# Weighting an expert's results by slot as they leave PSUM, adding them to x2's rows by accumulating gathers, and finishing the last tile in slot order

## The reference, cut to what matters

```python
x = x + hybrid_mixer(rms_norm(x, norm1_g), ...)       # x2 below
xn = rms_norm(x, norm2_g)
# router: best group, the two best experts in it, their weights
combine = sum(one_hot(expert_id, 16) * (g_w * top_p)[..., None], axis=1)
for e in range(16):
    h = silu(xn @ w_gate[e]) * (xn @ w_up[e])          # 1024 -> 512
    y = y + combine[:, e:e + 1] * (h @ w_down[e])      # 512 -> 1024
return rms_norm(x + y, final_norm_g)
```

## Time and profile before

| | |
|---|---|
| median of 3 runs | 788.62 us (787.97 to 789.51) |
| profiled execution, its own time | 789.02 us |
| its span | 787.3 us |
| busy: PE, DVE, ACT, POOL | 764.9 (97%), 492.3 (63%), 450.5 (57%), 209.3 (27%) us |
| DMA | 206.74 MB, mean 263 GB/s |

### The profile page before, as it was taken

The page is one execution under the profiler, slowest core; times in us unless marked ns, Lnnn a source line. Parts: engine busy times, 40 slices in busy tenths (PEclk is TensorE's granted clock), DMA queues, the critical chain, the costliest instruction groups (busy, mean ns, idle before and its releaser), DMA issues.

```text
span 787.3 us, 10839 instructions
## 1 busy us (share of the span) xinstructions
PE 764.9 (97%) x3739; PEld 621.8 (79%) x3739; DVE 492.3 (63%) x702; ACT 450.5 (57%) x590; POOL 209.3 (27%) x124
## 2 busy tenths in 40 slices
PE   7999999999999999999999999999999999999994
PEld 4788777777787888888888788878778888888782
DVE  5704476585743302322022669999999998999888
ACT  5244657566744232323321556787878888888862
POOL 3644433232332444434442532000000000000033
PEclk9999999999999999999999999999999999999998
DMA  8569999792222262332328438999999999999965
GB/s 300 183 213 381 370 337 393 268 342 75 69 66 81 81 214 87 100 107 81 107 97 282 161 131 285 408 409 409 409 409 409 410 409 410 409 409 341 398 251 202
DMA packets 134318, 206.74 MB, mean 263 GB/s; under 512 B 10813, under 2 KB 65669, under 8 KB 134278
## 3 DMA queue, kind: packets, MB, share of 16 engines
q1 hardware_dynamic: 126084, 188.80, 65.7%
q10 hardware_dynamic: 5890, 9.04, 3.1%
q0 software_dynamic: 2304, 8.39, 2.8%
HBM read 157.95 MB, written 48.25 MB: 262 GB/s over the span
## 4 chain that ended last, share of the span: by engine, by line
PE 85%; DVE 6%; ACTq 2%; DMA 2%; POOL 2%; ACT 1%; issue 1%; DVEq 0%; SPq 0%; POOLq 0%
PE ps L1052 25%; PE ps L1054 24%; PE ps L1053 24%; DVE w_lo L389 3%; PE ps L1342 2%; PE ps L1146 1%; PE ps L1174 1%; PE ps L1157 1%; PE ps L1295 1%; POOL raw_mg L656 1%; PE ps L1269 1%; DMA x<-in_x 1%; PE ps L1349 1%; ACTq L877 1%; DMA raw_mg<-slots,slot_idx 1%
## 5 line engine op out<-in xcount | busy, mean ns | idle before, releaser
L383 POOL TENSOR_TENSOR w_lo<-raw,w_hi 128x1024 fp32r<-128x1024 f32 x72 | 174.1, 2422 | 250.4 <-ACT w_hi L371 250.4
L371 ACT ACTIVATE w_hi<-raw 128x1024 fp32r<-128x1024 f32 x73 | 76.8, 1057 | 195.4 <-PE ps L1054 168.0
L1052 PE MATMUL ps<-xn_hi,w_hi 128*128 128x512 f32 x352 | 140.6, 399 | 0.0
L1054 PE MATMUL ps<-xn_hi,w_lo 128*128 128x512 f32 x352 | 137.2, 390 | 0.0
L1053 PE MATMUL ps<-xn_lo,w_hi 128*128 128x512 f32 x352 | 137.1, 390 | 0.0
L1052 PE MATMUL ps<-w_hi,xT_hi 128*128 128x512 f32 (+1 forms) x248 | 97.0, 391 | 2.2 <-DVE w_lo L389 2.2
L1054 PE MATMUL ps<-w_hi,xT_lo 128*128 128x512 f32 (+1 forms) x248 | 95.1, 384 | 0.0
L1053 PE MATMUL ps<-w_lo,xT_hi 128*128 128x512 f32 (+1 forms) x248 | 94.9, 383 | 0.0
L656 POOL DMA_INDIRECT raw_mg<-slots,slot_idx x7 | 7.8, 1113 | 280.4 <-DMA slots<-y_tile 278.5
L1052 PEld LDWEIGHTS ps<-xn_hi,w_hi 128*128 128x128 f32 x352 | 66.1, 188 | 16.2 <-issue 2.0
L1053 PEld LDWEIGHTS ps<-xn_lo,w_hi 128*128 128x128 f32 x352 | 66.1, 188 | 14.1 <-issue 1.0
(11 more groups left out here) (311 smaller groups left out, 1475.1 us busy)
## 6 DMA issues: line engine op xcount, KB each, us to landing
slots<-raw SPq DMA_DIRECT2D x65, 512.0 KB, 7.0
raw<-in_w_in SPq DMA_DIRECT2D x52, 512.0 KB, 4.0
raw_mg<-in_exp_w_down SPq DMA_DIRECT2D x35, 512.0 KB, 11.0
raw<-in_exp_w_gate SPq DMA_DIRECT2D x29, 512.0 KB, 11.3
raw_a<-in_exp_w_gate SPq DMA_DIRECT2D x26, 512.0 KB, 10.6
raw_c<-in_exp_w_up SPq DMA_DIRECT2D x24, 512.0 KB, 11.8
raw_mg<-in_exp_w_up SPq DMA_DIRECT2D x22, 512.0 KB, 11.9
raw<-in_exp_w_up SPq DMA_DIRECT2D x15, 512.0 KB, 11.8
```

What stands on the lines that cost most here:

```text
L371: nc.scalar.activation(w_hi[:, b % HI_SLOTS, :], raw_buf(b), ACT.Copy)\
L383: eng.tensor_tensor(w_lo[:, b % HI_SLOTS, :], raw_buf(b), w_hi[:, b % HI_SLOTS, :].bitcast(F32), ALU.subtract)\
L1052: pe.matmul(dst, hi_l, hi_r, start=start, stop=False)
L1054: return pe.matmul(dst, lo_l, hi_r, start=False, stop=stop)
```

## The change

- Each slot gets a record of four words in a DRAM tensor `info`: the token, its weight, the token's other slot, 0. POOL writes default records, then (once DVE has the weights) the picked slots' records by eight indirect writes, and loads all back to `slot_info`. DVE therefore makes the weights before tile 1.
- `y_part` multiplies by the slot's weight as it copies PSUM to the one buffer `y_home`. It waits for `info_in`. Tile 0's `y_part` comes three splits into the next tile.
- `last_rows_out` (DVE, after tile 4) finds which tokens have a slot in the last tile. POOL writes those tokens' x2 rows in slot order to DRAM (`last_x`) and loads them to `z_home`.
- No tile of zeros. POOL gathers with `compute_op=ALU.add` onto `x_rows`: four before the store of the tile before the last, four after it (and after the first four), and one onto `z_home`.
- The last tile's result is weighted from PSUM onto `z_home` in slot order and normed there; tokens in it are left out when `x_rows` is written. All output rows are written by POOL, by indirect DMA, in five parts.
- PE's and ACT's work with `sel` and the one-hot rows goes, and so do the sums on DVE.

The diff, cut to its core, in the order POOL, ACT, DVE (definitions, then the order of calls):

```diff
-SLOT_TILES = NE * PER_EXPERT + 1
+SLOT_TILES = NE * PER_EXPERT
...
+            pool.iota(slot_info[:, :, 0], pattern=[[0, SLOT_TILES]], base=TOK, channel_multiplier=1)
+            pool.memset(slot_info[:, :, 1:4], 0)
...
+            pool.dma_start(info.rearrange("(p b) n -> p (b n)", p=P), info_words).then_inc(S["info_filled"], 16)
...
             pool.wait_ge(S["routed"], NT + 1)
-            pool.wait_ge(S["y_even_stored"], 16 * (PAIRED // 2 + 1))
-            pool.wait_ge(S["y_odd_stored"], 16 * (PAIRED // 2))
+            for t in range(NT):
+                for k in range(2):
+                    pool.indirect_dma_start(
+                        info, bass.IndirectOffsetOnAxis(ap=info_idx[:, 0, 2 * t + k:2 * t + k + 1], axis=0),
+                        pick_info[:, t, k, :], None).then_inc(S["info_out"], 16)
+            pool.wait_ge(S["info_out"], 16 * 2 * NT)
+            pool.dma_start(info_words, info.rearrange("(p b) n -> p (b n)", p=P)).then_inc(S["info_in"], 16)
+            pool.wait_ge(S["routed"], NT + 2)
+            for t in range(NT):
+                pool.indirect_dma_start(last_x, bass.IndirectOffsetOnAxis(ap=last_places[:, t:t + 1], axis=0),
+                                        x_rows[:, t, :], None, bounds_check=P - 1, oob_is_err=False)\
+                    .then_inc(S["last_x_out"], 16)
...
+            pool.dma_start(z_home, last_x).then_inc(S["z_in"], 16)
...
+            def add_picked(rows, idx, landed_in):
+                pool.indirect_dma_start(rows, None, slots, bass.IndirectOffsetOnAxis(ap=idx, axis=0),
+                                        compute_op=ALU.add).then_inc(landed_in, 16)
+            pool.wait_ge(S["hT_hi_done"], n_stop + (PAIRED - 1))
+            pool.wait_ge(S["y_stored"], n_stop * 16 + 16 * (PAIRED - 1))
+            pool.wait_ge(S["info_in"], 16)
+            pool.tensor_copy(last_info[:, :], info_words[:, bass.ds(last_block * 4, 4)])
+            for t in range(NT):
+                add_picked(x_rows[:, t, :], slot_idx[:, 2 * t:2 * t + 1], S["early_in"])
...
             pool.wait_ge(S["before_last_stored"], 16)
+            add_picked(z_home, last_info[:, 2:3], S["z_in"])
+            pool.wait_ge(S["early_in"], 16 * NT)
             for t in range(NT):
-                gather(0, y_lo(t), t)
-                gather(1, y_hi(t), t)
+                add_picked(x_rows[:, t, :], slot_idx[:, 2 * t + 1:2 * t + 2], rows_in[t])
+            power(0)
+            power(1)
+            power(2)
+            rows_out(0)    
+            power(3)
+            rows_out(1)
+            power(NT)
+            rows_out(2)
+            pool.wait_ge(S["z_norm"], 2)
+            pool.indirect_dma_start(out[0], bass.IndirectOffsetOnAxis(ap=last_info[:, 0:1], axis=0), z_weighed, ...)
+            rows_out(3)
...
-                act.wait_ge(at.y_free, at.y_count)
-                act.activation(at.y, ps[:, 5:7, :].rearrange("p a n -> p (a n)"), ACT.Copy).then_inc(S["y_act"], 1)
+                act.wait_ge(S["info_in"], 16)
+                act.wait_ge(S["y_stored"], at.y_count)
+                act.activation(y_home, ps[:, 5:7, :].rearrange("p a n -> p (a n)"), ACT.Copy,
+                               scale=info_words[:, bass.ds(block * 4 + 1, 1)].bitcast(F32)).then_inc(S["y_act"], 1)
...
+                    if r == 2 and count == SECOND:
+                        y_part(loop_block(1, PER_TILE), at_odd(0), 0)
...
+            y_square(0)
+            y_square(1)
+            y_square(2)
+            z_square(0)
+            y_square(3)
+            z_square(1)
...
+            def info_rows():
+                at = info_idx[:, 0, :]
+                dve.wait_ge(S["routed"], NT)
+                dve.tensor_scalar(at, slot_idx[:, :], P - 1, 6, ALU.bitwise_and, ALU.logical_shift_left)
+                link(dve.tensor_scalar(info_idx[:, 1, :], slot_idx[:, :], 7, None, ALU.logical_shift_right))
+                link(dve.tensor_tensor(at, at, info_idx[:, 1, :], ALU.bitwise_or))
+            def share_of_picks():
+                dve.wait_ge(S["exp_done"], 2)
+                dve.tensor_reduce(g_sum, row(4, NT, NG), AX.X, ALU.add)
+                link(dve.tensor_tensor(mine, where.unsqueeze(2).to_broadcast([P, NT, 2, NE]),
+                                       top_slot[:, :, 0:2].unsqueeze(3).to_broadcast([P, NT, 2, NE]), ALU.is_equal))
+                link(dve.tensor_tensor(mine, mine, share.unsqueeze(2).to_broadcast([P, NT, 2, NE]), ALU.mult))
+                link(dve.tensor_reduce(w_both, mine, AX.X, ALU.add))
+            def last_rows_out():
+                both = top_slot[:, :, 0:2]
+                link(dve.tensor_scalar(in_last, both, last_rows[:, 0:1], None, ALU.is_gt))
+                link(dve.scalar_tensor_tensor(out=in_last, in0=both, scalar=last_rows[:, 1:2], in1=in_last,
+                                              op0=ALU.is_le, op1=ALU.mult))
+                link(dve.scalar_tensor_tensor(out=place_last, in0=both, scalar=last_rows[:, 0:1], in1=in_last,
+                                              op0=ALU.subtract, op1=ALU.mult))
+                link(dve.tensor_reduce(four(8), in_last, AX.X, ALU.add))
+                link(dve.tensor_reduce(four(9), place_last, AX.X, ALU.add))
+                dve.scalar_tensor_tensor(out=out_rows[:, :], in0=four(8), scalar=float(TOK), in1=pick_info[:, :, 0, 0],
+                                         op0=ALU.mult, op1=ALU.add)
...
+                dve.tensor_scalar(last_places[:, :], four(9), float(P), None, ALU.add).then_inc(S["routed"], 1)
+            def gather_order(before):
+                dve.tensor_scalar(before_rows[:, 0:1], block_table[:, bass.ds(before, 1)], float(P), None, ALU.mult)
+                link(dve.tensor_scalar(before_rows[:, 1:2], block_table[:, bass.ds(before, 1)], float(P), float(P),
+                                       ALU.mult, ALU.add))
...
+                dve.scalar_tensor_tensor(out=idx[:, :, 1], in0=at_second, scalar=-1.0, in1=apart,
+                                         op0=ALU.add, op1=ALU.subtract).then_inc(S["routed"], 1)
...
             overflow_count()
-            overflow_tiles(0, block_table, NE * PER_EXPERT)
+            share_of_picks()
             for r in range(AHEAD):
                 split_lo_loop(at_odd(0), r)
...
             hidden(B_EXP + 8, 1)
+            combine_weights()
...
             tile(at_odd(0))
+            overflow_tiles(0, block_table, NE * PER_EXPERT)
             full_tables()
+            tile(at_even(1))
             last_tile()
-            tile(at_even(1))
+            tile(at_odd(1))
             last_tile_rows()
-            gather_swaps()
-            tile(at_odd(1))
-            gather_order()
             tile(at_even(2))
-            share_of(0)
-            share_of(1)
+            last_rows_out()
             tile(at_odd(2))
-            combine_weights()
             dve.wait_ge(S["tab"], 1)
             n_stop = dve.value_load(tile_table[0:1, 0:1], ...)
+            gather_order(n_stop + (PAIRED - 1))
...
+            def z_sum(c):
+                at = slice(512 * c, 512 * (c + 1))
+                dve.wait_ge(S["w_used"], loop_block(tiles, 3 + c))
+                dve.scalar_tensor_tensor(out=z_home[:, at], in0=ps[:, 5 + c, :], scalar=last_info[:, 1:2].bitcast(F32),
+                                         in1=z_home[:, at], op0=ALU.mult, op1=ALU.add).then_inc(S["z_sum"], 1)
+            y_mean(0, 1)
+            y_normed(0)
+            y_mean(1, 2)
+            dve.wait_ge(S["z_in"], 32)
+            z_sum(0)
+            z_sum(1)
+            y_mean(2, 3)
+            y_normed(1)
+            z_weigh(0)
+            y_mean(3, 5)
+            z_weigh(1)
...
+            y_normed(2)
...
+            y_normed(3)
```

More of the change, by code:

```diff
@@ L300, in build @@
         x0_in = [sem(f"x0_in{s}") for s in range(NT)]
-        got_in = [[sem(f"got{k}_in{t}") for t in range(NT)] for k in range(2)]
+        rows_in = [sem(f"rows_in{t}") for t in range(NT)]
         even_buf = ([raw_a[:, n, :] for n in range(3)] + [raw_c[:, n, :] for n in range(4)] + [raw[:, 4, :]]
@@ new lines, in _ @@
+            pool.wait_ge(S["hT_hi_done"], n_stop + (PAIRED - 1))
+            pool.wait_ge(S["y_stored"], n_stop * 16 + 16 * (PAIRED - 1))
+            pool.wait_ge(S["info_in"], 16)
+            pool.tensor_copy(last_info[:, :], info_words[:, bass.ds(last_block * 4, 4)])\
+                .then_inc(S["consts_pool"], 1)
+            pool.wait_ge(S["routed"], NT + 3)
+            for t in range(NT):
+                add_picked(x_rows[:, t, :], slot_idx[:, 2 * t:2 * t + 1], S["early_in"])
+            pool.wait_ge(S["z_in"], 16)
@@ new lines, in power, with rows_out @@
+            def power(n):
+                at, mean = (stat[:, 7, n:n + 1], stat[:, 6, n:n + 1]) if n < NT else (stat[:, 4, 3:4], stat[:, 4, 2:3])
+                pool.wait_ge(S["y_stat"], n + 1)
+                pool.tensor_tensor(at, mean, minus_half[:, :], ALU.pow).then_inc(S["y_rstd"], 1)
```

(24 more changed lines are left out.)

254 lines of the change are left out of this document (94 added, 160 removed).

## The result

The changed kernel takes 802.01 us (801.26 to 802.56, 4 runs), the kernel before 788.96 (787.97 to 789.51, 4 runs): a ratio of 1.0166, interval 1.0149 to 1.0184, so 13.1 us slower. The forecast was 789.7, with a range from 784.5 to 795.5. The profiled execution took 801.26; its span is 799.1, which is 11.8 more than before.

What follows compares the result with a forecast made beforehand. PE was taken to pace the expert tiles (17.69 us each), a chain of waits the tail. Weights' wait 0.7, DVE's order 0.1 and tail 0.3 gave +1.1: 790.1 for the profiled execution, 789.7 as a median, range 784.5 to 795.5.

Steps and rivals of the forecast that it cites:

- Early adds ... I take the middle, 1.92: Tail: four accumulating gathers onto x2, 1.92 us each between bounds 1.28 and 2.56, seen landed at 763.9.
- an add has some room: Tail, argument against half rate: eight plain gathers move 358 of 410 GB/s, so issuing holds them more than DMA.
- Adds at half rate: Slower rival, tail: each add costs 2.56 us, last landing 779.7, +5.1 in all, 793.7; chance 0.22.
- No stall if info_in comes by 516.3; 517.3; I take 0.7.: Tile 2: ACT's wait for slots' weights, info_in expected at 517.3, costs 0.7 us; bounds 0 and 15.
- The prediction's sign for being wrong: Tile 2: forecast is wrong if PE idles over 2 us near 515 to 520.
- DVE's order: net +0.1.: Front tiles: 0.9 us late ahead of tile 1, later gaps cost 2.9 instead of 3.7; bounds -0.8 and +1.5.
- its gap less about 0.9 us: Between tiles: DVE's routing arithmetic makes a tile late by its gap minus about 0.9 us.
- New traffic: 0.: Loop: about 1.2 MB of rows and infos cost 0, as early weight loads cover it; without cover 2.9 us.
- After them ... +0.3.: Tail after last landing: ACT's squares, POOL's five powers and five indirect output writes end near 787.6, +0.3 us.
- The faster rival, 784.4,: Tail: adds at 1.28 us, last rows landed at 771.5, POOL's ops short, 784.4 with front cost; chance 0.28.

Runs made afterwards that it cites:

- the first form with fewer adds: Kernel after with tile 0's rows weighed later, infos' fill later, routing inside tiles, four late adds made plain gathers summed by DVE: 798.33 us, ratio 1.0117.

## Why the prediction was wrong

**The failed step: "Early adds ... I take the middle, 1.92 (three streams of data instead of two), as no row is nearer."** An add costs what the upper bound said: the landings are 2.48 to 2.65 us apart, and POOL issues an add every 2.5 to 2.7 (early) or 1.85 (late) instead of 1.46. I had two bounds, 1.28 for one read and 2.56 for two, and took a value between them that stands for neither. The argument against the upper one (358 of 410 GB/s, so "an add has some room") was right that issuing held the plain gathers, but the room was 0.2 us each (1.46 less 1.28), far from the 1.28 that a second read would need. The kernel before with adds shows that price alone: 9.6 us for eight.

**The size of it.** The rival "Adds at half rate" had the mechanism and 793.7, and is still 8.3 us short. 1.6 of these lie between the profiled executions and the medians; its span would be 787.3 + 5.1 = 792.4, and 799.1 were measured, 6.7 more. They divide so:

- 2.0: the front is 2.8 late at the turn at 738.83, where 0.8 was forecast.
- -0.7: from that turn to the first add's issue it takes 15.7 us, where the rival had 16.3.
- 3.1: from that issue to the landing of the early ones it takes 17.1 us (754.50 to 771.6), where the rival had 14.0.
- 1.1: from there to the last landing it takes 14.4 us, where the rival had 13.3. The first late add lands 6.4 us after its issue, where 4.7 was taken, and meanwhile the DMA side runs dry.
- 1.2: from the last landing to the end it takes 13.1 us, where the rival had 11.9.

z's add, which the prediction put at no cost between early and late ones, is not among them: issued at 764.53, it lands at 774.1, 2.5 us behind the last early one, in the time in which the late ones are only being issued. The 3.1 us lie ahead of it. In the run where each late add waits for its own rows, the third early add lands 15.0 us after the first one's issue (768.8 and 753.81), where the rival had 11.4, and from it on the landings are 2.5 us apart. The store of the tile before the last (issued at 757.65, landed 5.0 later) flows in this stretch too. That it and the late start of the first transfers make the 3.1 us is argued, and in what shares stays open.

**"No stall if info_in comes by 516.3; 517.3; I take 0.7."** The wait and its place were right, the size was not. (The rule itself gives 1.0 at 517.3.) The weights came at 518.9, because the eight indirect writes of the infos, priced as the earlier trace rows at 1.46 each, ran from 495.96 to 509.4, 1.68 each. By the rule (518.95 - 516.3) that is 2.6; tile 2 lost 2.5, and lost nothing when the weighing moved. The prediction's sign for being wrong, PE idle over 2 us near 515 to 520, was met nearly to the place: 2.25 us up to 522.92.

**"DVE's order: net +0.1."** 0.9 was forecast to be lost ahead of tile 1, and 0.9 was, between the turns near 487 and near 503. For tiles 3 to 6 the forecast was 0 + 0 + 0.7 + 1.8 = 2.5 instead of 3.25 in the kernel before. They lost 0.65 + 0.35 + 0.60 + 0.48 = 2.1 (turns at 524.42, 542.76, 560.80, 579.09 and 597.26, less 17.69 each). So the sum is near partly by luck: "its gap less about 0.9 us" holds for tile 5 only. Tiles 3 and 4 should have taken 17.7 us and took 18.34 and 18.04; tile 6 should have lost 1.8.

**"New traffic: 0."** It holds: from 614.95 to 738.83 seven tiles take 123.88 us, and 123.86 before.

**"After them ... +0.3."** From the last landing to the last write's start I had 7.8 us, and it took 8.06; to the end I had about 12, and it took 13.1. Of the five writes one was long to issue (1.90 us), the others took 0.96 to 1.23. So this row of POOL's was priced about right, but as a swap: I set it against DVE's row of sums in the kernel before (13.3), and nothing was gained. The run with SP's stores shows that this row costs 5 us against plain stores (without the last tile's rows).

**The faster rival, 784.4,** needed plain prices for the adds. With them, and with the weighing later and the rows stored by SP, the kernel takes 785.65 (part of the work left out). So the idea of fetching the first pick early hangs on an add's price; a complete kernel that has it was not made.

## What to carry to other kernels

An accumulating gather onto SBUF ran at half the rate of a plain one here. At a tail where the DMA side ends last, moving a sum from an idle DVE (1.2 us for 512 KB) to the DMA side (1.3 us more for 512 KB, one behind another) gains nothing. When a cost has two bounds from a mechanism (one read or two), ask which mechanism applies and take its bound instead of the middle. A transfer that is started "early" on the queue that the late ones need is brought forward only if that queue has a hole as long as the transfer: here four early adds cost 7.7 us, and even plain early gathers slowed the store on which the next one waited (5.8 instead of 2.6 us to land).

## What the runs showed of the hardware

- Accumulating gathers of 128 rows of 4 KB move 195 to 210 GB/s at a full DMA side. Plain ones move 340 at a share of 0.91, and 411 at a full side. Issue on POOL takes 1.54 us at least against 0.94.
- A plain gather issued right behind five adds (at 764.75, in the first form with fewer adds) is landed 10.2 us later, against a median of 5.8 in the kernel before. The rate stays at 213 GB/s up to 770 and is 411 from 772.5 on: the plain ones flow behind the adds.
- In one run an indirect write of 512 KB put among the adds went with a next landing 1.5 us later.
- In the kernel after, PE has no work from 775 us on, and the clock granted there is 0.50 (1.2 GHz); it was 1.00 up to 770, while PE was busy. It costs nothing.
